# A Toeplitz block copied by group, down tiles over eight PSUM banks, and finer hand-overs in a two-layer trunk

## What is computed

```
for l in range(2):
    sh1, sc1, g1, sh2, sc2, g2 = split(silu(c) @ w_ada[l] + b_ada[l])      # six rows of 1024
    h = rms_norm(x) * (1 + sc1) + sh1
    u, cq, ckv, kr, gate_a, gate_b = split(h @ w_in[l])                    # 512, 256, 128, 32, 1024, 1024
    y = gelu(C @ scan(A, B @ u) + d * u)                                   # 32 groups of 16 channels, 64 complex states
    y_a = (y * sigmoid(y @ w_glu[l])) @ w_a_out[l]
    y_b = causal_attention(cq, ckv, kr) @ w_b_out[l]                       # 8 heads, low-rank q and kv, rotary part
    x = x + g1 * ((sigmoid(gate_a) * y_a + sigmoid(gate_b) * y_b) @ w_out[l])
    h = rms_norm(x) * (1 + sc2) + sh2
    x = x + g2 * ((silu(h @ w_gate[l]) * (h @ w_up[l])) @ w_down[l])       # 2816 wide
return rms_norm(x)
```

## Time and profile before

| | |
|---|---|
| median of three executions | 3154.01 us (3153.0 to 3155.38) |
| the profiled execution | 3150.09 us |
| its span, first to last instruction | 3147.9 us |
| mean granted clock of TensorE | 0.987 of full speed |
| TensorE matmuls busy | 3044.4 us, 97% of the span |
| TensorE weight loads busy | 2559.9 us, 81% |
| VectorE / ScalarE / GpSimd busy | 1546.8 / 986.5 / 870.6 us |
| DMA | 264.25 MB, mean 84 GB/s |

### The profile page before, as it was taken

The page is one execution under the profiler, slowest core; times in us unless marked ns, Lnnn a source line. Parts: engine busy times, 40 slices in busy tenths (PEclk is TensorE's granted clock), DMA queues, the critical chain, the costliest instruction groups (busy, mean ns, idle before and its releaser), DMA issues.

```text
span 3147.9 us, 36605 instructions
## 1 busy us (share of the span) xinstructions
PE 3044.4 (97%) x14672; PEld 2559.9 (81%) x14672; DVE 1546.8 (49%) x1949; ACT 986.5 (31%) x1397; POOL 870.6 (28%) x512
## 2 busy tenths in 40 slices
PE   6999999999999999999999999999999999999998
PEld 5787889978878888888878888898787888888886
DVE  7865487855133232232379885786524222232224
ACT  3422367751231111111142225777223111111112
POOL 0334222222422222222244542222232222222223
PEclk9999999999999999999999999999999999999999
DMA  7555400124221222111125651002331111111111
GB/s 269 170 157 156 154 13 12 51 61 155 79 75 61 62 78 63 61 61 47 47 101 168 187 175 55 14 25 51 121 135 40 51 50 47 47 47 47 48 53 67
DMA packets 278932, 264.25 MB, mean 84 GB/s; under 512 B 46706, under 2 KB 237298, under 8 KB 277619
## 3 DMA queue, kind: packets, MB, share of 16 engines
q1 hardware_dynamic: 252464, 217.66, 22.7%
q10 hardware_dynamic: 26306, 44.32, 3.8%
HBM read 218.59 MB, written 40.96 MB: 82 GB/s over the span
## 4 chain that ended last, share of the span: by engine, by line
PE 80%; DVE 7%; issue 5%; ACT 4%; DMA 2%; POOL 1%; SPq 1%; ACTq 1%; DVEq 0%; POOLq 0%
PE ps L550 22%; PE ps L552 22%; PE ps L553 21%; PE ps L1321 3%; PE ps L1307 2%; PE ps L1341 2%; PE ps L1342 2%; PE ps L1302 2%; PE ps L1306 2%; DVE x_sb L2420 1%; DVE silu L2402 1%; DMA raw<-in_w_in 1%; ACT hid_hi L1536 1%; PE ps L1186 1%; PE ps L1168 1%
## 5 line engine op out<-in xcount | busy, mean ns | idle before, releaser
L534 POOL TENSOR_TENSOR wlo<-raw,whi 128x1024 fp32r<-128x1024 f32 (+3 forms) x288 | 543.4, 1895 | 1963.6 <-ACT whi L526 1963.6
L526 ACT ACTIVATE whi<-raw 128x1024 fp32r<-128x1024 f32 (+3 forms) x290 | 242.8, 859 | 1637.5 <-PE ps L553 1480.5
L550 PE MATMUL ps<-h_hi,whi 128*128 128x512 f32 x2176 | 701.0, 396 | 25.8 <-DVE h_lo L2042 18.2
L552 PE MATMUL ps<-h_lo,whi 128*128 128x512 f32 x2176 | 692.3, 392 | 0.0
L553 PE MATMUL ps<-h_hi,wlo 128*128 128x512 f32 x2176 | 691.7, 392 | 0.0
L550 PEld LDWEIGHTS ps<-h_hi,whi 128*128 128x128 f32 x2176 | 409.3, 190 | 114.3 <-DVE h_lo L2042 22.2
L552 PEld LDWEIGHTS ps<-h_lo,whi 128*128 128x128 f32 x2176 | 412.8, 190 | 86.7
L553 PEld LDWEIGHTS ps<-h_hi,wlo 128*128 128x128 f32 x2176 | 411.8, 189 | 87.4
L2402 DVE TENSOR_TENSOR silu<-silu,ps 128x1024 f32<-128x1024 f32 x44 | 53.7, 1221 | 769.4 <-PE ps L553 760.2
L2420 DVE SCALAR_TENSOR_TENSOR x_sb<-ps,mod,x_sb 128x1024 f32<-128x1024 f32 x160 | 203.2, 1280 | 178.0 <-PE ps L553 178.0
L550 PE MATMUL ps<-hid_hi,whi 128*128 128x512 f32 x704 | 224.8, 393 | 9.5 <-DVE x_sb L2420 9.5
(11 more groups left out here) (250 smaller groups left out, 4250.9 us busy)
## 6 DMA issues: line engine op xcount, KB each, us to landing
ada_raw<-in_w_ada SPq DMA_DIRECT2D x64, 512.0 KB, 4.5
raw<-in_w_in SPq DMA_DIRECT2D x92, 256.0 KB, 4.7
raw<-in_w_gate SPq DMA_DIRECT2D x88, 256.0 KB, 3.2
raw<-in_w_up SPq DMA_DIRECT2D x88, 256.0 KB, 3.3
raw<-in_w_down SPq DMA_DIRECT2D x88, 256.0 KB, 2.8
gate_scratch<-gst ACTq DMA_DIRECT2D x32, 512.0 KB, 3.8
gl<-gate_scratch SPq DMA_DIRECT2D x32, 512.0 KB, 4.1
ada_rows<-in_w_ada SPq DMA_DIRECT2D x16, 512.0 KB, 5.6
```

What stands on the lines that cost most here:

```text
L526: last = act.activation(dst(whi[:, s, :]), src(raw[:, s, :]), ACT.Copy)
L534: last = pool.tensor_tensor(dst(wlo[:, s, :]), src(raw[:, s, :]), dst(whi[:, s, :].bitcast(F32)), ALU.subtract)
L550: pe.matmul(o, w_h, x_h, start=first, stop=False)
L552: pe.matmul(o, w_h, x_l, start=False, stop=False)
```

## The change

The Toeplitz block of a batch is copied by ScalarE into `toe_g`, with each group's weights dense, and the outputs use the copy (`batch_by_group`, part 2 of a batch; `toe_ready`). On ScalarE part 2 comes behind the split of the same step, part 0 ahead of it as before. The `ut` loads go one step later on SP in layer 0, so that they follow the next gate unit; in layer 1 they stay. Down tiles go round over all eight banks. The merge takes the `yg` tiles one by one. Three low weight parts go from GpSimd to VectorE (`weight_lo`): units `U_FFN + 1` and `U_FFN + 2`, and `U_U + 1` in layer 1. The return of x comes as two DMAs. The first attention step has no projection beside it, the next three have what the first three had. The split of the first gate unit goes ahead of the exponential in the mixer's parameters, their sine behind two copies of u. The last mean of squares is made from seven summed tiles and the eighth by itself. The store of the last batch's outputs goes behind the latents' high parts.

```diff
@@ -286,6 +286,7 @@
 d_col = sb("d_col", [P, G, M])
+toe_g = sb("toe_g", [P, 4, CH, M])
@@ -442,6 +443,7 @@
 toe_loaded = count("toe_loaded", 16 * CH * 8)
+toe_ready = count("toe_ready", 8)
@@ -457,7 +459,7 @@
 mg_ready = count("mg_ready", KT)
-x_back = count("x_back", 16)
+x_back = [count("x_back_first", 16), count("x_back_rest", 16)]
@@ -585,7 +587,7 @@
         if i == 0:
-            return ((VS, 0, 1), (KO, 0, 0), (KO, 0, 1), None, None, None)[g]
+            return (None, (VS, 0, 1), (KO, 0, 0), (KO, 0, 1), None, None)[g]
@@ -728,8 +730,9 @@
                 ada_pair(t - 3)
-            if t >= 3 and t % 2 and (t - 3) // 2 < 8:
-                ut_load((t - 3) // 2)
+            b, odd = divmod(t - 1 - S5_LAG[l] // 2, 2)
+            if 0 <= b < 8 and not odd:
+                ut_load(b)
@@ -1052,23 +1055,21 @@
         add_squares(l, 1, 1, KT - 2)
-        split_lo(pool, l, U_FFN + 1)
         add_squares(l, 1, 1, KT - 1)
+        wait(pool, w_lo_done, l, U_FFN + 3)
...
             for j in range(6):
-                split_lo(pool, l, U_FFN + 2 + j, 3 * i)
-        for n in range(UNITS - 4, UNITS):
+                split_lo(pool, l, U_FFN + 3 + j, 3 * i)
+        for n in range(UNITS - 3, UNITS):
...
             add_squares(l + 1, 0, 0, k)
-        for k in range(1, KT):
+        for k in range(1, KT if l + 1 < DEPTH else KT - 1):
...
             add_squares(l + 1, 0, 1, k)
-        if l + 1 < DEPTH:
-            split_lo(pool, l + 1, U_U + 1)
@@ -1177,13 +1178,13 @@
             wait(pe, mat_step, l, 6 * b + 6)
-            wait(pe, toe_loaded, l, 16 * CH * (b + 1))
+            wait(pe, toe_ready, l, b + 1)
...
                 o = ps[:, 7, g * P:(g + 1) * P]
-                pe.matmul(o, toe[:, j, :, :, g].rearrange("p r m -> p (r m)"), ut[:, j, g, :], start=True, stop=False)
+                pe.matmul(o, toe_g[:, g, :, :].rearrange("p r m -> p (r m)"), ut[:, j, g, :], start=True, stop=False)
@@ -1403,10 +1404,10 @@
                 tile_products(pe, j, 4 * j + 2, o_hi, o_lo, [(4 + k, k)], first=(k == 0), last=(k == PAIRS - 1))
-            if t == 0:
-                wait(pe, yg_ready, l, 4)
-            end = tile_products(pe, j, 4 * j, yg_hi, yg_lo, [(k, k) for k in range(4)])
+            for k in range(4):
+                if t == 0:
+                    wait(pe, yg_ready, l, k + 1)
+                end = tile_products(pe, j, 4 * j, yg_hi, yg_lo, [(k, k)], first=(k == 0), last=(k == 3))
@@ -1445,10 +1446,11 @@
                             pe.wait_ge(up_done.sem, up_done.at(l, 2 * c_static - 1) + c_reg * 2)
+                            pe.wait_ge(dn_ev.sem, dn_ev.at(l, 8 * (c_static - 2) + 5 + w_i) + c_reg * 8)
+                        else:
+                            pe.wait_ge(up_done.sem, up_done.at(l, 2 * c_static) + c_reg * 2)
                             pe.wait_ge(dn_ev.sem, dn_ev.at(l, 8 * (c_static - 2) + 7 + w_i) + c_reg * 8)
-                        else:
-                            pe.wait_ge(up_done.sem, up_done.at(l, 2 * c_static) + c_reg * 2)
@@ -1459,13 +1461,12 @@
                     t = 4 * d + nn
-                    b = 2 * (t % 2)
-                    if t < 2:
-                        pe.wait_ge(up_done.sem, up_done.at(l, 2 * c_static + (2 if last_chunk else 3)) + c_reg * 2)
-                        pe.wait_ge(dn_ev.sem, dn_ev.at(l, 8 * (c_static - 1) + 7 + t) + c_reg * 8)
+                    b = 2 * (t % 4)
+                    if t < 4:
+                        pe.wait_ge(up_done.sem, up_done.at(l, 2 * c_static + 3 + t // 2) + c_reg * 2)
                     else:
-                        pe.wait_ge(dn_ev.sem, dn_ev.at(l, 8 * c_static + t - 1) + c_reg * 8)
+                        pe.wait_ge(dn_ev.sem, dn_ev.at(l, 8 * c_static + t - 3) + c_reg * 8)
@@ -1516,7 +1517,7 @@
-                wait(pe, dn_ev, l, 8 * last_chunk + (n - 3 if n >= 4 else n // 2 - 1))
+                wait(pe, dn_ev, l, 8 * last_chunk + (n - 3 if n >= 4 else n // 2 - 3))
@@ -1527,7 +1528,15 @@
-    mean_squares(DEPTH, 1)
+    wait(pe, sq_added[1], DEPTH, KT - 2)
+    for part in range(2):
+        if part:
+            wait(pe, sq_ready[1], DEPTH, KT)
+        for t in range(4, TT):
+            rows = (sq_sum[:, t * P:(t + 1) * P], sq_ring[:, 2 + (KT - 1) % 2, (t - 4) * P:(t - 3) * P])[part]
+            last = pe.matmul(ps[:, 6, t:t + 1], rows, mean_col[:, :], start=(part == 0 and t == 4),
+                             stop=(part == 1), skip_group_check=True)
+    last.then_inc(sq_mm.sem, 1)
@@ -1607,13 +1616,14 @@
                 mask_block(k)
+        split_hi(act, l, U_GATE)
...
         act.activation(sm[:, S_MAG:S_MAG + 2, :], sm[:, S_AD:S_AD + 2, :], ACT.Exp).then_inc(s5_act.sem, 1)
-        wait(act, s5_dve, l, S5_ANGLES_READY)
-        act.activation(trig[:, :, :], sm[:, 0:6, :], ACT.Sin).then_inc(s5_act.sem, 1)
-        split_hi(act, l, U_GATE)
...
         for n, (ct, side) in enumerate(U_ORDER):
+            if n == 2:
+                wait(act, s5_dve, l, S5_ANGLES_READY)
+                act.activation(trig[:, :, :], sm[:, 0:6, :], ACT.Sin).then_inc(s5_act.sem, 1)
@@ -1635,12 +1645,20 @@
+        def batch_by_group(b):
+            wait(act, toe_loaded, l, 16 * CH * (b + 1))
+            copy(toe_g[:, :, :, :], toe[:, b % 2, :, :, :].rearrange("p r m g -> p g r m")).then_inc(toe_ready.sem, 1)
...
                            ACT.Gelu_apprx_tanh).then_inc(y_gelu.sem, 1)
+            if b < 7:
+                outputs_away(b)
+        def outputs_away(b):
@@ -1654,13 +1672,18 @@
                     batch_toeplitz(b)
+                elif part == 2:
+                    batch_by_group(b)
...
         for t in range(2 * KT):
-            s5_part(2 * t)
-            if t < 2 * KT:
-                split_hi(act, l, U_GATE + t + 2)
+            turn = (2 * t - S5_LAG[l]) % 4
+            if turn == 0:
+                s5_part(2 * t)
+            split_hi(act, l, U_GATE + t + 2)
+            if turn == 2:
+                s5_part(2 * t)
@@ -1703,14 +1726,15 @@
         latent(2)
-        s5_part(4 * KT + 5)
...
         latent_rms(1)
+        s5_part(4 * KT + 5)
...
         latent_hi(2)
+        outputs_away(7)
@@ -1835,11 +1859,15 @@
         wait(act, x_spilled, l, 16)
-        act.dma_start(x_sb[:, :, :], xs_dram).then_inc(x_back.sem, 16)
+        for part, tiles in enumerate((slice(0, 2), slice(2, KT))):
+            act.dma_start(x_sb[:, tiles, :], xs_dram[:, tiles, :]).then_inc(x_back[part].sem, 16)
...
             wait(act, wo_ev, l, n + 1)
+            if n == 0:
+                for part in x_back:
+                    wait(act, part, l, 16)
@@ -2018,6 +2046,14 @@
+    def weight_lo(l, n):
+        s = n % 2
+        wait(dve, w_hi_done, l, n + 1)
+        wait(dve, w_lo_done, l, n)
+        apart(dve)
+        lo_of(wlo[:, s, :], raw[:, s, :], whi[:, s, :]).then_inc(w_lo_done.sem, 1)
@@ -2059,6 +2095,8 @@
+        if l:
+            weight_lo(l, U_U + 1)
@@ -2362,9 +2400,10 @@
-        wait(dve, x_back, l, 16)
-        apart(dve)
         for n in range(KT - 2):
+            if n in (0, 2):
+                wait(dve, x_back[n // 2], l, 16)
+                apart(dve)
@@ -2385,7 +2424,9 @@
         last_out(KT - 1, 1)
-        for k in range(1, 6):
+        hidden_lo(l, 2, 1)
+        weight_lo(l, U_FFN + 1)
+        for k in range(2, 6):
@@ -2393,6 +2434,7 @@
             hidden_lo(l, 3, k)
+        weight_lo(l, U_FFN + 2)
@@ -2417,7 +2459,7 @@
                 dve.wait_ge(dn_ev.sem, dn_ev.at(l, 8 * (c_static - 1) + t + 1) + 8 * c_reg)
-                dve.scalar_tensor_tensor(x_sb[:, t, :], pair(2 * (t % 2)), mod[:, 5, t:t + 1], x_sb[:, t, :],
+                dve.scalar_tensor_tensor(x_sb[:, t, :], pair(2 * (t % 4)), mod[:, 5, t:t + 1], x_sb[:, t, :],
```

More of the change, by code:

```diff
@@ L1447, in up_products @@
                                     pe.wait_ge(up_done.sem, up_done.at(l, 2 * c_static - 1) + c_reg * 2)
-                                    pe.wait_ge(dn_ev.sem, dn_ev.at(l, 8 * (c_static - 2) + 7 + w_i) + c_reg * 8)
+                                    pe.wait_ge(dn_ev.sem, dn_ev.at(l, 8 * (c_static - 2) + 5 + w_i) + c_reg * 8)
                                 else:
                                     pe.wait_ge(up_done.sem, up_done.at(l, 2 * c_static) + c_reg * 2)
+                                    pe.wait_ge(dn_ev.sem, dn_ev.at(l, 8 * (c_static - 2) + 7 + w_i) + c_reg * 8)
                             end = tile_products(pe, u % 2, b, h_hi, h_lo, [(k, k) for k in range(KT)])
```

## The result

The changed kernel takes 3188.39 us (3187.48 to 3192.46), the kernel before on the same chip 3154.7: a ratio of 1.0108, with a 95% interval of 1.0091 to 1.0126. It is slower by 34 us where I forecast 10, and lies 0.4 us above my range. The profiled execution has a span of 3186.2 us against 3147.9, a difference of 38.3: 4.6 more than that of the medians, chiefly since the profiled execution of the kernel before (3150.09) lies that far under its median of 3154.7.

What follows compares the result with a forecast made beforehand. TensorE, busy nearly throughout, was taken as the bound, with idle time and slow clock in layer 0's mixer. Copy waits outweighed the savings: +10.5 us on 3150.09 gave 3160.6, or 3164 us as a median, range 3143 to 3188.

Steps and rivals of the forecast that it cites:

- Toeplitz copy, layer 0: Layer 0 mixer: outputs wait 9.5 us for the copy behind the split, 37.9 us a batch over six batches, +47.7.
- Layer 1: Layer 1 mixer: outputs wait 1.9 us for split, copy and hand-over in seven batches, +13.2; the strided read separately +2.0.
- the clock stays up: Layer 1 mixer: waits of 1.9 us in 28 leave TensorE at full clock; its ends allowed one or two falls, +3.
- Starts: Layer 0 gate start: TensorE 4.7 us earlier, then waiting for batch 0's ut, landing about 152; -1.2 in all.
- Last batch of layer 0: Layer 0 mixer: the step between batches 6 and 7 loses part of its present stall, -1.5.
- Norm 2: Second norm: VectorE makes the low weight part, k=2 starts about 1.7 us earlier, half the slow clock credited; -9.0 over both layers.
- Attention: Attention start: no value half in step 0, so transposes come 2.7 us earlier; -5.4, ends -2 and -7.
- Down tiles, merge, sums: Eight-bank down tiles -15.0; yg tiles one by one at the merge -9.9; last sums, layer 1's first sums and latents -3.4.
- A: Rival, layer 0: gate unit lands in time, issued 7.5 us earlier, six waits 2.0 and not 9.5; 3105 us, chance 0.10.
- B: Rival, both layers: the copy is free, running under the gate unit; 3078 us, chance 0.05.
- C: Rival: half the hand-overs' gain lost (+14), lower clock after each of layer 1's seven waits (+12); 3190 us, chance 0.12.
- 29 us of hand-overs: Gains forecast at merge, norm, attention and starts, 29 us together, half of which C took to be lost.

Runs made afterwards that it cites:

- Copy ahead: The changed kernel with ScalarE's Toeplitz copy ahead of the split of the same step: 3119.32 us, 0.9898 of the kernel before.
- copy alone: The kernel before with only the Toeplitz copy added, behind the split, ut loads at their old place: 3229.42 us, ratio 1.0252.
- dense read: The changed kernel with the copy reading the Toeplitz block as it lies, outputs not the reference's: 3177.36 us, 1.0083 of the kernel before.
- best kernels: Copy ahead of split, stores behind mt, early sine, other norm 2 order; successively batch 0's ut back, all ut back, first spread early: 3104.74, 3094.96, 3091.39 us.
- the stores alone: The changed kernel with copy ahead of the split, plus a batch's output stores behind the next mt copy: 3120.12 us, 0.9898 of before.
- the loads alone: The changed kernel with copy ahead of the split, plus all layer 0 ut loads at their old place: 3111.84 us, 0.9871 of before.
- the two starts as before: The changed kernel with batch 0's layer 0 ut loads and layer 1's sine back at their old places: 3175.33 us, 1.0079 of before.

## Why the prediction was right in kind and too low

The direction was right and the size was not. Two steps of the prediction failed most. Layer 1's wait for the copy was put at 1.9 us with the clock staying up; it was 2.43, and the clock fell behind four of the seven, 9.1 us more. The place of the sine in layer 1 was put at nothing and cost 4.7. That is half of the 27.8 us between +10.5 and +38.3; the rest lies at the start and the last batch of layer 0 (3.7 and 4.4), in norm 2 (4.0) and in the attention (4.1), less about 2 where it came out better. Two terms are also rounded amiss: seven waits of 1.9 are 13.3 and three times 1.1 is 3.3, so that the sum should read +10.7.

*Toeplitz copy, layer 0: right.* In the third batch the split starts at V+20.5 (forecast V+20.65) and the outputs at V+22.7 (V+22.3; 0.5 of stride came on top). The six steps take 37.95 in the mean, for 37.9 and 0.15 of stride. That the total fits so well is in part luck. The stride cost 0.5 and not 0.15 a copy, and the first step took 39.4; against that, the clock cost 1.9 a step and not 2.3 (from outputs to next V 15.2 us, where a step of layer 1 at full clock has 13.3). Copy ahead and copy alone show the cause from both sides: program order on ScalarE, behind a split that waits for a load.

*Layer 1: the step that failed.* I wrote split, copy, hand-over, 1.9 us, and "the clock stays up". The place was right; two sizes were not. The wait is 2.43, by the stride: I took 0.75 us for the copy with an upper end of 0.95, and it is 1.11. The dense read shows 0.62 for the same size, a factor of 1.8. (The Trainium skill, "SBUF — State Buffer", section "Door 1: The DMA port swizzle": the trace agrees that such a read pays, and for more than my upper end. No run has a shorter stride, so none shows that the 16-byte line is the reason.) And at 2.43 us the clock falls behind four of seven waits, 1.61 each, while at 1.93 it falls behind none. So the forecast's sentence holds for the wait that it forecast. The two sizes are worth 2.7 and 6.4 us. The outputs gained 0.76 a batch behind the wait, for 0.75 forecast.

The kernel before had a warning that I read past. Two of its four waits for `mt` are of 2.5 us; the clock stays up behind the first and falls behind the second. The two waits, then the windows behind them:

```profile
243.15 0.38 PE L1168 MATMUL ps<-ut,mt 128*128 128x128 f32 x1 [2.52 <-ACT mt L1536]
272.68 0.53 PE L1168 MATMUL ps<-ut,mt 128*128 128x128 f32 x1 [2.51 <-ACT mt L1536]
```
```profile
243.20:250.00 6.80, 6.80 (x38) 5.94 (x39) 5.52 (x7) 3.15 (x3) 5.80 (x4) 1.00 0.25 90
272.80:279.60 6.80, 6.80 (x24) 6.06 (x25) 4.72 (x6) 3.08 (x3) 5.87 (x4) 0.50 0.27 96
```

*Starts: I followed the change in one layer only.* In layer 1 the move of the sine cost 4.7 us (3.1 of wait, 1.6 of clock). I had named the sine among the edits and costed its place nowhere. In layer 0 I did follow the `ut` loads, and put their landing at 152 from the issues of before; in the changed kernel the w_ada pair ahead of them is issued from 146.99 and not from 143.56, so they were issued 149.67 to 152.3, and TensorE got them at 155.69.

*Last batch of layer 0.* The seventh step lost 1.6, for 1.5 forecast. But the gate unit's load was late by then (ScalarE's split waits 9.09 us for it, until 404.05), and TensorE waited 2.71 us for `mt`, with the clock low for 10.2 us behind it; I had followed `mt` for no batch after the change.

*Norm 2: about half.* VectorE made the weight part in 1.22, and GpSimd's addition beside it took 2.76. VectorE's next operation then took 1.75 in place of 0.75:

```profile
911.80 1.22 DVE L1944 TENSOR_TENSOR wlo<-raw,whi 128x1024 fp32r<-128x1024 f32 x1
912.94 1.75 DVE L2068 SCALAR_TENSOR_TENSOR t_ring<-x_sb,a,rb 128x512 f32<-128x512 f32 x1
```
```profile
911.38 2.76 POOL L910 TENSOR_TENSOR sq_sum<-sq_sum,sq_ring 128x512 f32<-128x512 f32 x1 [4.31 <-ACT sq_ring L1557]
```

So 1.0 is lost in each layer (the same two durations stand in layer 1). (The Trainium skill, "SBUF — State Buffer", section "SBUF: two separate sides": an exclusive lock on a shared pair of ports. These rows agree with it: GpSimd's addition, most often 1.29 us, ends 1.2 us after VectorE's next operation was due. No run took the addition away.) That wait was not new. The kernel before has it in the same place:

```profile
869.20 1.76 DVE L2032 SCALAR_TENSOR_TENSOR t_ring<-x_sb,a,rb 128x512 f32<-128x512 f32 x1
```

With it, the third product of the first unit came 1.0 us earlier and not 1.7, in both layers: 1.4 of the miss of 4.0. The clock is the larger part. I credited 1.7 in each layer. In layer 0 the lower level fell from 6.8 us to 3.4, from 914.9 on, which gave about 0.9; in layer 1 it stayed at 6.8, from 2444.1 on, and gave nothing. It went in both layers only with the other order of products in the best kernels, where TensorE has work ready while it waits for the third `h_lo`.

*Attention: half, and half of that lost again.* ScalarE's table load waits for VectorE's maximum, and the exponential stands behind both:

```profile
467.01 1.28 ACT L1807 ACT_TABLE_LOAD   x1 [0.94 <-DVE neg_max L2368]
468.30 1.11 ACT L1807 ACTIVATE probs<-ps,neg_max 128x1024 f32<-128x1024 f32 x1
```

Before, that maximum was there at 415.63 and the load began behind the value half's copy:

```profile
416.17 0.60 ACT L1536 ACTIVATE v_st<-ps 128x512 fp32r<-128x512 f32 x1 [1.38 <-PE ps L1283]
416.78 1.28 ACT L1783 ACT_TABLE_LOAD   x1
```

So 1.15 us was about all that the value half's place could give, and 1.3 came. I had added up what was removed and not asked what was ready. In layer 1 TensorE then waits 1.0 us for `pt_lo` near the end of the attention, where the kernel before did not, and 1.3 are lost again. The kernel with the copy alone has the attention of the kernel before and lost 1.9 at the same place, so the new order need not be the reason; it stays open.

*Down tiles, merge, sums: right.* -15.8 for -15.0, 0.79 a chunk, with no wait for an eviction left; merge -10.1 for -9.9.

*The rivals.* A needed the gate unit 7.5 us earlier; it landed as late as forecast (split at V+20.5). B needed the copy out of the split's way, which is what the copy-ahead kernel does. C described the miss best: of the 29 us of hand-overs 10.1 + 5.0 + 1.3 + 1.7 + 1.0 came, and 2.5 and 4.7 were paid at the two starts, so 17 were lost, and the clock fell in layer 1, though behind four waits and not seven. I gave it 0.12.

## What to carry to other kernels

Before an edit puts an instruction on the path of the busiest engine, read what stands ahead of it in its own engine's queue and what that waits for; here the same copy costs 1.9% of the time behind a split, against the change without it, and saves some 0.25% ahead of it, which is little more than the measurement can tell. Follow each moved instruction in every layer in which it moves, and for each wait that is taken away look up when the next input was really ready. Where two inputs end last by turns, taking away one shows little: in the six steps of layer 0 the stores alone and the loads alone changed the 183.6 us by less than 2, both together, with the other edits of the last kernels, by 9.

## What the runs showed of the hardware

A ScalarE copy of 128x512 float32 that reads every fourth element takes 1.11 us, a dense one 0.60 to 0.62. After waits of TensorE of 2.43 us in a step of 28 its granted clock fell to the lower level for 3.4 us in four cases of seven in the changed kernel, and in five of seven in the one with the two starts as before and in the one with the copy alone, though the waits of one kernel are alike; after 1.93 us it fell in none of seven. Waits of like length were followed by lower stretches of unlike length: none and 6.8 us after two of 2.5 us in the kernel before, 10.2 us after one of 2.71 in the changed one.
